# Long convolution on one core: filter samples on four quarter tiles of TensorE, PSUM banks dealt anew

## What is computed

```python
def hyena_filter(L, ...):                    # samples of the filter, per channel
    ...
    h = h @ w_o.astype(f32)                  # (L,64) @ (64, 2*D): forward and backward halves
    h_fwd = h[:, :D_A] * decay
    h_bwd = h[:, D_A:] * decay
    l1 = jnp.sum(jnp.abs(h_fwd), axis=0) + jnp.sum(jnp.abs(h_bwd[1:]), axis=0)
    k = jnp.concatenate([h_fwd, jnp.zeros((1, D_A), f32), h_bwd[1:][::-1]], axis=0)
    return k / (l1[None, :] + EPS)

def long_conv_bidir(u, k, skip):
    U = jnp.fft.rfft(uf, n=2 * L, axis=1)
    K = jnp.fft.rfft(k, axis=0)
    y = jnp.fft.irfft(U * K[None], n=2 * L, axis=1)[:, :L]
    return (y + uf * skip.astype(jnp.float32)).astype(u.dtype)
```

## Time and profile before

| | |
|---|---|
| median of 3 runs | 3100.89 us (3099.92 to 3102.55) |
| profiled execution | 3099.8 us; its span 3098.0 us |
| mean granted clock of TensorE in it | 0.989 |
| PE busy in it | 2977.7 us, 96% |
| DVE busy in it | 2477.7 us, 80% |
| ACT busy in it | 870.9 us, 28% |
| long convolution, first sample to last inverse product | 2221.6 to 2736.6 us |

### The profile page before, as it was taken

How to read it: one execution, slowest core, us unless ns; L and a number is a source line. 1 busy time by engine, 2 the same in 40 slices (tenths; PEclk the granted TensorE clock), 3 DMA queues, 4 the chain that set the end, 5 groups by cost and what they waited for, 6 DMA issues and landing times. The chain is left out here.

```text
span 3098.0 us, 33135 instructions
## 1 busy us (share of the span) xinstructions
PE 2977.7 (96%) x12866; PEld 2161.9 (70%) x12866; DVE 2477.7 (80%) x2746; ACT 870.9 (28%) x1449; POOL 381.8 (12%) x512
## 2 busy tenths in 40 slices
PE   8999999999998999999999999999899999889999
PEld 4444444656776888888888888887656666678887
DVE  7979999898996888999899999998478979862221
ACT  3000000596334331111121211112444735731111
POOL 2212121001343441011000000000000100000000
PEclk9999999999999999999999999999999999999999
DMA  7576553301447547777666566652322331454231
GB/s 217 171 178 166 170 148 90 116 1 59 143 157 243 173 134 193 196 194 185 172 168 160 149 177 163 160 157 70 113 92 82 111 122 41 150 180 124 84 109 41
DMA packets 218869, 430.53 MB, mean 139 GB/s; under 512 B 21872, under 2 KB 135192, under 8 KB 210840
## 3 DMA queue, kind: packets, MB, share of 16 engines
q1 hardware_dynamic: 189256, 324.58, 34.9%
q0 software_dynamic: 28304, 95.44, 12.4%
q10 hardware_dynamic: 1152, 8.39, 0.7%
HBM read 324.53 MB, written 85.98 MB: 133 GB/s over the span
## 5 line engine op out<-in xcount | busy, mean ns | idle before, releaser
L1898 PE MATMUL PS<-HX,WH 128*128 128x512 f32 x1536 | 599.2, 390 | 6.9 <-DVE MB L1780 5.0
L1899 PE MATMUL PS<-HX,WH 128*128 128x512 f32 x1536 | 598.3, 390 | 0.0
L1900 PE MATMUL PS<-HX,WL 128*128 128x512 f32 x1536 | 598.2, 389 | 0.0
L849 PE MATMUL PS<-M 128*128 128x512 f32 x1088 | 472.2, 596 | 8.1 <-DVE M L650 6.8
L849 PEld LDWEIGHTS PS<-M 128*128 128x128 f32 x1088 | 207.3, 191 | 272.8 <-issue 263.5
L1898 PEld LDWEIGHTS PS<-HX,WH 128*128 128x128 f32 x1536 | 288.9, 188 | 67.9 <-DVE MB L1780 5.9
L120 DVE SCALAR_TENSOR_TENSOR HP<-MF,HP 128x1024 f32<-128x1024 f32 x252 | 323.5, 1284 | 14.1 <-DMA MF<-h_scratch 5.9
L1900 PEld LDWEIGHTS PS<-HX,WL 128*128 128x128 f32 x1536 | 288.7, 188 | 60.1
L1899 PEld LDWEIGHTS PS<-HX,WH 128*128 128x128 f32 x1536 | 288.8, 188 | 59.7
L120 DVE SCALAR_TENSOR_TENSOR M<-M 128x1024 f32<-128x1024 f32 x160 | 205.6, 1285 | 27.4 <-DMA M<-c_feat 21.8
L2591 PE MATMUL PS<-WH,YH 128*128 128x512 f32 x512 | 202.1, 395 | 9.3 <-DVE HP L2730 5.2
(11 more groups left out here) (230 smaller groups left out, 5085.9 us busy)
## 6 DMA issues: line engine op xcount, KB each, us to landing
MF<-h_scratch SPq DMA_DIRECT2D x380, 256.0 KB, 5.1
M<-c_feat POOLq DMA_DIRECT2D x186, 256.0 KB, 4.3
MF<-w_in SPq DMA_DIRECT2D x52, 512.0 KB, 4.5
WL<-MF POOLq DMA_DIRECT2D x46, 512.0 KB, 4.5
M<-u_scratch SPq DMA_DIRECT2D x16, 1024.0 KB, 4.9
M<-c_decay POOLq DMA_DIRECT2D x48, 256.0 KB, 2.9
M<-x SPq DMA_DIRECT2D x18, 512.0 KB, 4.2
M<-w_in SPq DMA_DIRECT2D x18, 512.0 KB, 5.3
```

The costliest lines, as they stand in the source:

```text
L849: ins = t.matmul(ps[:, c, :], wt[:, k], HT[:, k, TC * c:TC * c + TC], start=(k == 0), stop=(k == KD - 1))
L1898: t.matmul(dst, wh, hh, start=(k == 0), stop=False)
L1899: t.matmul(dst, wh, hl, start=False, stop=False)
L1900: ins = t.matmul(dst, wl, hh, start=False, stop=(k == KD - 1))
```

## The change

- **Samples.** The products of the odd column (x = 1) go to the other half of the partitions: the forward side lands in partitions 64 to 127, the backward side in 0 to 63. With the even column's two, the four products stand on all four 64x64 tiles of the array. The two columns lie in two neighbouring banks now (4/5 or 6/7 for the samples of chunk 0, 6/7 for all others), 256 columns in each. The table of decays is exchanged in the same way.
- **First stage of the filter's FFT.** Since odd columns have their sides exchanged, they need a matrix with its halves exchanged (`AF_SWAPPED`, a new constant with a DMA of its own). The one product over 512 columns becomes two over 256, one for even and one for odd columns; each reads single columns and writes every second column of the bank.
- **Banks.** The forms have two pairs, 0/1 and 2/3, in place of three; the inverse has two banks, 4 and 5, in turn, in place of one; the samples have 6/7.
- **Waits that follow.** `forms(p)` waits for the product of bin p - 2 in place of p - 3; `inverse(n)` waits for the copy of bin n - 2 in place of n - 1; the wait of `forms(2)` for the gate's readings goes, and the first two inverses of a chunk have it.

```diff
         def banks_of(n):
-            return 2 * (n % 16 % 3), 2 * (n % 16 % 3) + 1
+            return 2 * (n % 2), 2 * (n % 2) + 1
...
-        def sample_bank(kq):
-            return 6 + kq % 2 if kq < 16 else 7
+        def sample_place(kq):
+            bank = 4 if kq < 16 and kq % 2 else 6
+            return PS[:, bank:bank + 2, 0:CH]
+
+        def inverse_bank(n):
+            return 4 + n % 2
...
                 for x in range(2):
                     for d in range(2):
                         p = slice(HID * d, HID * d + HID)
-                        ins = t.matmul(PS[p, sample_bank(kq), CH * x:CH * x + CH], h3[p, 2 * j + x], WOC[cc % 2][p],
-                                       start=True, stop=True)
+                        to = HID * (d if x == 0 else 1 - d)
+                        ins = t.matmul(sample_place(kq)[to:to + HID, x], h3[p, 2 * j + x], WOC[cc % 2][p], start=True, stop=True)
...
-                    t.matmul(PS[:, n % 4, :], AF, KTC[cc % 2][:, 16 * g:16 * g + 16], start=True, stop=True).then_inc(ak_done, 1)
+                    formed = PS[:, n % 4, :].rearrange("p (c a y) -> p c a y", a=16, y=2)
+                    for y, forward in enumerate((AF, AF_SWAPPED)):
+                        ins = t.matmul(formed[:, :, :, y], forward, KTC[cc % 2][:, 16 * g:16 * g + 16, :, y], start=True, stop=True)
+                    ins.then_inc(ak_done, 1)
...
                 t.wait_ge(y_done, n + 1)
-                if n:
-                    t.wait_ge(z_done, n)
-                if bp == 0:
-                    t.wait_ge(l1_read, n // 8 + 2)
-                    if n:
-                        t.wait_ge(yc_done, n // 2)
+                if n >= 2:
+                    t.wait_ge(z_done, n - 1)
+                if bp < 2:
+                    t.wait_ge(l1_read, n // 16 * 2 + 2)
+                    if n >= 16:
+                        t.wait_ge(yc_done, n // 16 * 8)
...
                     n = 16 * cc + p
-                    if p >= 3:
-                        t.wait_ge(pm_done, n - 2)
-                    if p == 2 and cc:
-                        t.wait_ge(yc_done, 8 * cc)
+                    if p >= 2:
+                        t.wait_ge(pm_done, n - 1)
```

More of the change, by code:

```diff
@@ L1957, in long_convolution @@
         AI = region(41472, HID)
+        AF_SWAPPED = region(41552, P)
         SKIP = region(41536, KD)
@@ L2070, in _ @@
             channels_in(0)
-            for dst, name in ((AF, "c_fwd"), (AFU.rearrange("p a b -> p (a b)"), "c_fwd_u"), (AI, "c_inv"),
+            for dst, name in ((AF, "c_fwd"), (AFU.rearrange("p a b -> p (a b)"), "c_fwd_u"), (AI, "c_inv"), (AF_SWAPPED, "c_fwd_swapped"),
                               (SKIP, "hyena_skip_2"), (IDENT, "c_ident")):
@@ L2161, in inverse_out @@
                 s.wait_ge(inv_done, n + 1)
-                s.activation(UTB[:, n % 16], PS[:, 6, :].rearrange("p (y c) -> p y c", y=2), ACT.Copy).then_inc(z_done, 1)
+                s.activation(UTB[:, n % 16], PS[:, inverse_bank(n), :].rearrange("p (y c) -> p y c", y=2), ACT.Copy).then_inc(z_done, 1)
             decays(0)
@@ L2168, in _ @@
                 absolute(kq)
-            s.wait_ge(const2_in, 16 * 5)
+            s.wait_ge(const2_in, 16 * 6)
             inputs_out(0)
@@ L2231, in weighted @@
                 out = KB[cc % 2][:, 512 * j:512 * j + 512]
-                v.tensor_tensor(out.rearrange("p (c x) -> p x c", x=2), PS[:, sample_bank(kq), :].rearrange("p (x c) -> p x c", x=2),
+                v.tensor_tensor(out.rearrange("p (c x) -> p x c", x=2), sample_place(kq),
                                 DEC[kq % 4].rearrange("p (x c) -> p x c", x=2), ALU.mult).then_inc(k_weighted, 1)
@@ L2441, in inverse @@
                 t.wait_ge(y_done, n + 1)
[L2442 to L2447 removed]
+                if n >= 2:
[4 more added lines that the diff above has]
+                        t.wait_ge(yc_done, n // 16 * 8)
                 for x in range(2):
[L2449 removed]
+                    ins = t.matmul(PS[:, inverse_bank(n), CH * x:CH * x + CH], INV[:, 2 * bp + x], UTB[:, bp, x],
                                    start=True, stop=True)
@@ L2496, in _ @@
                 generate(kq)
-            t.wait_ge(const2_in, 16 * 5)
+            t.wait_ge(const2_in, 16 * 6)
             filter_first(0)
@@ L2880, in constants @@
     c["c_tneg"] = np.ascontiguousarray(-pos[at].reshape(P, 32))
+    c["c_tneg"][:, 1::2] = np.roll(c["c_tneg"][:, 1::2], HID, axis=0)
+    c["c_fwd_swapped"] = np.roll(c["c_fwd"], HID, axis=0)
     lo, hi = math.log(1e-2) / 1.5, math.log(1e-2) / 0.3
```

## The result

The changed kernel takes 3191.78 us (median of four runs, 3191.10 to 3194.55), the kernel before in the same series 3101.36 (3099.92 to 3102.55): ratio 1.0289, 95% interval 1.0269 to 1.0310. It is slower by 90 us, where 37 were forecast. The profiled execution has a span of 3190.4 against 3098.0.

The account below looks back on a forecast made before the run. PE was taken to bound the kernel, DVE 0.04 us a bin behind, and a new two-bin loop to bind after the change. Terms 17.9 + 14.9 + 4 + 1.2 - 1 = +37.0 us gave 3138, range 3118 to 3190.

Parts of the forecast that it names:

- PE sets the pace before, DVE is 0.04 behind: Second stage, kernel before: PE's period is 3.98 us a bin, DVE alone 3.94, so relieving PE gains at most 0.04.
- The loop over two bins: Second stage, chunks 0 to 2: forms wait for the product two bins back, 8.76 us per two bins, +17.9 in all.
- The 1.6 of the clock: Chunks 1 and 2, second stage: 1.6 us more than chunk 0 where the granted clock fell, kept in the forecast.
- The last chunk without the clock, +14.9: Last chunk's second stage: the loop takes 8.25 us for two bins, first to last product 61.6 against 46.7.
- The clock in the last chunk, +4: Last chunk's second stage: a few falls of the granted clock while PE is idle, +4 us.
- The bound of +20: Upper bound and rival: all of the last chunk at the lower clock, +20 in place of +4, 3154 us; chance 0.10.
- The first stage of the filter, +1.2: Two 256-column products a group: records of 0.218 to 0.24 us, +0.6 in chunk 0 and +0.2 in each other chunk.
- the rival: Filter's first stage: stepped PSUM writes make 256-column records take 0.436 us, chunk 0's stage 27.9, total 3188; chance 0.20.
- The upper end of the range, 3190: Whole kernel: range 3118 to 3190 us, taking in the forecast, slow stepped writes and low clock, leaving some 0.15 out.
- Samples, −1: Chunk 0's own samples: four tiles together save between 0 and 2.9 us of DVE's wait for PE, taken as -1.

Follow-up runs that it names:

- banks alone: The kernel before with only the change's banks and waits, samples still on two tiles and the filter's first stage as it was: 3146.71 us (before 3098.12).
- all repairs: The changed kernel with channels innermost and inverse ahead of forms: 3109.95 us; also chunk 0's sample products issued twice: 3109.26; also a third bank pair in the last chunk: 3109.13.
- one variant: The changed kernel with the first stage's channels innermost and the inverse ahead of the forms, sample products issued once: 3109.95 us, ratio 1.0027.
- pairs: The changed kernel with first-stage products reading pairs of neighbouring values, still writing every second column (filter's transform left wrong): 3154.41 us (before 3098.12).
- near reads: The changed kernel with channels innermost in the first stage, so single values read are 8 B apart and writes step by 128 B: 3153.86 us (before 3100.98).
- samples twice: The changed kernel with channels innermost and inverse ahead of the forms, plus chunk 0's sample products issued twice on four tiles: 3109.26 us, ratio 1.0032.

## Why the prediction missed

The direction, the bound and the mechanism of the second stage were right; the sum was 54 us short.

- **PE sets the pace before, DVE is 0.04 behind.** Right. With PE relieved and the loop cut, the bins come at 3.93 (3.94 forecast), and four tiles bring no more over the kernel before.
- **The loop over two bins.** Right, and to the step: 8.73 for 8.76, the forms 0.06 after the third product for 0.09, first to last product with the banks alone 65.0 and 66.6 for 65.3 and 66.8. The term was +17.9. With the banks alone it is +17.1. In the changed kernel it is +20.6; the 3.5 more are one more fall of the clock in chunk 0 (66.6 against 65.0) and one of 6.8 us in place of 3.4 in chunks 1 and 2 (67.6 and 67.5 against 66.6). The 1.6 of the clock that I kept in for chunks 1 and 2 came with the banks alone too (66.6 against 65.0).
- **The last chunk without the clock, +14.9.** Right within about 1.5 us: 61.6 forecast, 62.9 and 63.0 where few falls remain.
- **The clock in the last chunk, +4.** The size was off: 8 (81.9 against 74.0). I took a few falls, each of about a bin, from rows where PE was idle once. Here PE is idle ahead of every pair of bins, and the clock falls in nearly every pair. The bound of +20 held it.
- **The first stage of the filter, +1.2: this is the step that failed.** "A 256-column record takes 0.218 if it is half of that, and 0.24 by the eight of the forms in 1.92." It takes 0.434, and the term is +50.7. The row from which I priced it, the forms, reads values 8 B apart; the changed product reads values 2 KB apart. The other price, half of a 512-column record, was of reads in pairs of neighbours; 0.218 comes back when pairs are read. I had named both unknowns, the stepped write and the far single reads, in one sentence, and then wrote the rival and its chance on the writes alone. With the reads slow the first stage takes 28.8 to 29.0, near the 27.9 of that rival, whose other terms stood: so its 3188 came close to the 3191.78 by luck, with a mechanism that the runs refute. The upper end of the range, 3190, was this rival's time with 2 us to spare, and it had no room for this rival and more falls of the clock together, which is what happened.
- **Samples, −1.** −0.7, but not shown to come from the tiles: two tiles on the new banks take 24.5 too. DVE waits for PE 0.7 us in all there in the changed kernel, 1.2 with the banks alone, 2.9 before. The four tiles run together (0.73 for 1.13), but I hadn't thought that this may keep the clock low: it is why chunk 0's first stage takes 17.4 with its reads mended. In the changed kernel the slow reads cover it, since they go as fast at 0.50.
- **Still open.** After all repairs 9 us remain (3109 against 3100 to 3101). 2.4 of them are chunk 0's clock in one variant, yet with that mended the median stayed. Falls of 17 us came in four profiled executions (banks alone, pairs, near reads, samples twice in the inputs of chunk 1 or 3), always 3.4 to 3.6 us behind the last start of a first stage, with PE busy in all of the low stretch. In the 4 us ahead of the fall PE was busy 3.2, and so it was at the same place in chunks 1 and 2 of the kernel before, whose clock stayed. So the profiles show neither what starts them nor why the kernel before is spared. That the clock is all of the 9 us was not shown.

## What to carry to other kernels

Splitting one product into two that each take every second value looks like the same number of columns, yet the moving operand's step in SBUF can double its time: price a record by a row with the same distance between the values read, and if there is none, choose the loop order in which neighbours are near. When a buffer is taken from a ring, list what is queued behind the new wait on its engine; with the inverse behind the wait it cost 44 us here, with the inverse ahead of it and four tiles 1.7. The order has its own price, though: in the kernel before, with two tiles and PE as the bound, it cost 8 us in three stages. And an engine that has been given less to do may be given a lower clock, so what was saved there can come back in the next stage.

## What the runs showed of the hardware

- Single fp32 values 2 KB apart as the moving operand: 0.434 us per record of 256 columns, at a granted clock of 0.50 and at 1.00 alike. Pairs, or single values 8 B apart: 0.218 at 1.00 and 0.427 at 0.50.
- Writing fp32 to PSUM in steps of 8 B or of 128 B: no cost seen (0.218 a record in both, at 1.00).
- Four products on the four 64x64 tiles take 0.73 us where two at a time took 1.13; with them the clock stayed at 0.50 for 30.7 us in chunk 0 (34.1 in two of the kernels), and it stayed for 6.8 before, with the banks alone and with the products issued twice.
- The granted clock fell to 0.50 for 17 us in four profiled executions, in stretches where PE was busy in 4.00 of each 4 us.
